# A two-block transformer kernel: vector products that move from TensorE to VectorE, low parts that move to GpSimd, and shorter waits in both mixers

## What is computed

```python
mod = silu(c) @ w_ada + b_ada                 # 2048 x 12288, per block
h = rms_norm(x, g) * (1 + scale1) + shift1
x = x + gate1 * (mixer(h @ w_in) @ w_out)     # block 1: retention, RWKV-7, MoBA
h = rms_norm(x, g) * (1 + scale2) + shift2    # block 2: Fourier mix, mLSTM both ways
u = depthwise_conv3(h @ w_up)                 # 2048 x 11264
x = x + gate2 * ((silu(gate) * value) @ w_down)
```

## Time and profile before

| | |
|---|---|
| runs (3), median, lowest to highest | 2574.45 us, 2573.42 to 2577.0 |
| the profiled execution: time, span | 2573.34 us, 2571.5 us |
| PE busy | 2504.7 us (97%) |
| DVE, ACT, POOL busy | 1410.7 (55%), 1121.8 (44%), 1227.0 (48%) us |
| DMA | 611.69 MB, mean 238 GB/s |
| mean granted clock of PE | 0.992 |

### The profile page before, as it was taken

How to read it: one execution, slowest core, us unless ns; L and a number is a source line. 1 busy time by engine, 2 the same in 40 slices (tenths; PEclk the granted TensorE clock), 3 DMA queues, 4 the chain that set the end, 5 groups by cost and what they waited for, 6 DMA issues and landing times.

```text
span 2571.5 us, 50484 instructions
## 1 busy us (share of the span) xinstructions
PE 2504.7 (97%) x19860; PEld 2284.6 (89%) x19860; DVE 1410.7 (55%) x2324; ACT 1121.8 (44%) x1316; POOL 1227.0 (48%) x500
## 2 busy tenths in 40 slices
PE   7999999999999999999999999999999999999997
PEld 5887887889999999998888877899999999998886
DVE  2535224465776777776665635345765756443333
ACT  2253324444444444444444444443544444444443
POOL 2663444665444444444444565466443444434442
...
GB/s 396 391 245 158 198 198 197 254 308 287 237 271 277 277 262 265 273 271 261 272 265 257 161 234 191 188 255 302 191 217 246 222 234 192 181 183 193 191 191 120
DMA packets 140382, 611.69 MB, mean 238 GB/s; under 512 B 15584, under 2 KB 15968, under 8 KB 115680
## 3 DMA queue, kind: packets, MB, share of 16 engines
...
...
## 4 chain that ended last, share of the span: by engine, by line
issue 45%; PE 32%; POOL 20%; DMA 1%; POOLq 1%; DVE 1%; ACT 0%; DVEq 0%; SPq 0%; ACTq 0%
PE psum L1927 32%; POOL wlo L1736 20%; DMA raw<-wstream 1%; POOLq L1733 0%; DMA ada_raw<-adastream 0%; DVE xT L2266 0%; POOLq L1735 0%; PE psum L2156 0%; ACT whi L1747 0%; DVE psum L2266 0%; DVE gslo L2258 0%; ACT arena L1750 0%; ACT gshi L1747 0%; POOLq L1736 0%; ACT arena L1747 0%
## 5 line engine op out<-in xcount | busy, mean ns | idle before, releaser
L1736 POOL TENSOR_TENSOR wlo<-raw,whi 128x1024 fp32r<-128x1024 f32 x496 | 1226.8, 2479 | 1315.7 <-ACT whi L1747 1314.8
L1747 ACT ACTIVATE whi<-raw 128x1024 fp32r<-128x1024 f32 x760 | 800.5, 1059 | 957.3 <-PE psum L1927 732.5
L1927 PE MATMUL psum<-hi_h,whi 128*128 128x256 f32 x4224 | 1207.1, 286 | 7.0 <-POOL wlo L1736 4.0
L1927 PE MATMUL psum<-hi_h,wlo 128*128 128x256 f32 x4224 | 1191.4, 282 | 0.0
L1927 PE MATMUL psum<-lo_h,whi 128*128 128x256 f32 x4224 | 1191.2, 282 | 0.0
L1927 PEld LDWEIGHTS psum<-hi_h,whi 128*128 128x128 f32 x4224 | 799.5, 189 | 20.0 <-issue 6.7
L1927 PEld LDWEIGHTS psum<-hi_h,wlo 128*128 128x128 f32 x4224 | 799.7, 189 | 1.9 <-issue 1.7
L1927 PEld LDWEIGHTS psum<-lo_h,whi 128*128 128x128 f32 x4224 | 799.4, 189 | 0.0
L2258 DVE TENSOR_TENSOR wlo<-raw,whi 128x1024 fp32r<-128x1024 f32 x264 | 378.6, 1438 | 280.1 <-ACT whi L1747 280.1
L2266 DVE SCALAR_TENSOR_TENSOR psum<-ada_raw,cact,psum 128x256 f32<-128x256 f32 x702 | 287.5, 481 | 15.5 <-DMA ada_raw<-adastream 15.4
L1927 PE MATMUL psum<-whi,gshi 128*128 128x512 f32 x704 | 276.7, 393 | 3.9 <-DVE gslo L2258 3.5
...
## 6 DMA issues: line engine op xcount, KB each, us to landing
raw<-wstream SPq DMA_DIRECT2D x760, 512.0 KB, 4.6
ada_raw<-adastream SPq DMA_DIRECT2D x168, 1024.0 KB, 7.1
arena<-adastream SPq DMA_DIRECT2D x24, 1024.0 KB, 17.7
xT<-x_in SPq DMA_DIRECT2D x8, 512.0 KB, 6.5
y_out<-xT SPq DMA_DIRECT2D x4, 512.0 KB, 2.6
gs_pages<-tabs_in SPq DMA_DIRECT2D x2, 512.0 KB, 4.3
gs_pages<-rw_in SPq DMA_DIRECT2D x2, 512.0 KB, 7.2
...
```

What stands on the lines that cost most here:

```text
L1736: nc.gpsimd.tensor_tensor(wlo[:, q, :], raw[:, q, :], whi[:, q, :].bitcast(F32), ALU.subtract).then_inc(sem.lo_ready, 1)
L1747: return nc.scalar.activation(out_, in_, ACT.Copy, scale=scale)
L1927: return nc.tensor.matmul(o, lhsT, rhs, start=start, stop=stop, skip_group_check=True)
```

## The change

- **Units in mixer 1.** `LOOP_UNITS` are units 19 to 26, two for each of the four turns. PE multiplies them no longer; DVE does, in `loop_products`, one instruction depending on the one before, in slices of 1 to 12 between the levels. PE keeps the `finish` of each.
- **Mixer 2 has none.** Its nine units are made in FFN 1 up, where nine of eleven turns (`UP_UNITS1`) now have three units. The three finishes of such a turn stand ahead of slab 6, ahead of slab 12, and at its end.
- **POOL makes all low parts of FFN 1 up**; DVE starts with FFN 1 down.
- **Waits.** Mixer 1: ACT makes two `whi` before it waits for the first low-rank product; MoBA's normalisation of four heads is shared by ACT (two) and DVE (two), and PE waits by head. A `fill(1)` moves from before the last `t_ready` to the end of the turn. Mixer 2: two slabs go ahead of the gates; the reciprocal and what follows it in a head use PSUM bank 6 in place of SBUF. Both FFNs: ACT and DVE split the first two chunks of the down product's input earlier.

```diff
-SPOTS2 = (12, 16, 20, 24, 32, 40, 48, 56, 64)
+LOOP_UNITS = (START_UNITS + 3, START_UNITS + 11)
+UP_UNITS1 = ((1, 2), (9, 3), (1, 2))
...
 def by_pe(u):
-    return u < MIX_UNITS1[1] or MIX_UNITS2[0] <= u < MIX_UNITS2[1]
+    return u < LOOP_UNITS[0] or LOOP_UNITS[1] <= u < MIX_UNITS1[1]
...
-    if n % 2 and (B1_UP <= n < B2 or n >= B2_UP):
+    if n % 2 and (B1_DOWN <= n < B2 or n >= B2_UP):
         return True, dve
...
                 scores_of(1, bank[6], 0, sem.sc2)
                 fill(1)
+                spot()
...
-                    if l == 2:
+                    if l == 4:
                         spot()
-                fill(1)
                 pe.wait_ge(sem.t_ready, 6 * t + 6)
...
                 ins.then_inc(sem.fh, 1)
-                spot()
+                fill(1)
...
             def moba_turn(n):
-                pe.wait_ge(sem.mo_p, n + 1)
                 for h in range(4):
                     o = bank[(6, 4, 5, 6)[h]]
+                    pe.wait_ge((sem.mo_p_act, sem.mo_p)[h // 2], 2 * n + 1 + h % 2)
...
             fn(halves(3)[:, 1, :], halves(3)[:, 1, :], ACT.Sigmoid).then_inc(sem.lora_act, 1)
+            his(G_TQK * GS + 3, G_TQK * GS + 5)
             act.wait_ge(sem.lora_pe, 1)
...
                     dve.wait_ge(sem.u_done, 5 * t + l)
                     if l < 5:
                         tt(MT, L1T, level(l + 1), ALU.mult).then_inc(*at.up(sem.mt))
-                    if l == 3:
-                        unit_rows()
+                    loop_products(*{1: (2 * t, 0, 3), 2: (2 * t, 5, 8), 3: (2 * t, 10, 13), 4: (2 * t, 15, 16),
+                                    5: (2 * t + 1, 0, 4)}[l])
                     dve.wait_ge(sem.d_done, 5 * t + l)
...
+                    loop_products(*{1: (2 * t, 3, 5), 2: (2 * t, 8, 10), 3: (2 * t, 13, 15), 4: (2 * t, 16, 16),
+                                    5: (2 * t + 1, 4, 16)}[l])
...
+            slot(1, 0)
             pe.wait_ge(sem.wg_ready, 1)
...
             ins.then_inc(sem.gates, 1)
-            slot(1, 0)
             slot(1, 1)
+            slot(1, 2)
 
             pe.wait_ge(sem.gt_ready, 1)
...
-                    tt(inv, inv, bank[5], ALU.max).then_inc(*at.up(sem.step))
+                    tt(inv, least, bank[5], ALU.max).then_inc(*at.up(sem.step))
                     dve.wait_ge(*at.last)
                     V.reciprocal(inv, inv).then_inc(*at.up(sem.step))
                     dve.wait_ge(*at.last)
-                    for n, (pp, jb, q, d) in enumerate(PARTS):
-                        tt(pp, pp, inv[:, d * S + q.start:d * S + q.stop], ALU.mult).then_inc(*at.up(sem.step))
+                    fwd0, bwd1 = inv[:, 0:S], inv[:, S:2 * S]
+                    tt(pf0, pf0, fwd0, ALU.mult).then_inc(*at.up(sem.step))
...
-                        if t == NFF - 1 and half == 1:
+                        if t == NFF - 1 and half == 0:
                             for kk in range(2):
                                 gs_hi(n0 + more * NFF, b, kk)
...
+                            if units == 3 and k == (6, 4)[half]:
+                                finish(0, units * per, 0 if i is None else i)
...
+            def loop_products(n, k0, k1):
+                u = LOOP_UNITS[0] + n
+                for kt in range(k0, k1):
+                    s, k = divmod(kt, 8)
+                    if k == 0:
+                        dve.wait_ge(sem.ada_landed[s], 16 * (u - START_UNITS + 1))
+                    w, c = ada_raw[:, s, k * 256:(k + 1) * 256], cact[:, kt:kt + 1]
+                    if kt == 0:
+                        dve.wait_ge(sem.ada_sum, u)
+                        ts(sums_of(0), w, c, None, ALU.mult).then_inc(*at.up(sem.step))
+                    else:
+                        dve.wait_ge(*st["sum"])
```

More of the change, by code:

```diff
@@ L134, in ada_places @@
         first = spots[u - units[0] - 1] + 4 if u > units[0] else spot - 6
+        late = LOOP_UNITS[0] <= u < LOOP_UNITS[1] and (u - LOOP_UNITS[0]) % 2
         for s in range(2):
-            at.setdefault(n0 + first + s, []).append((u, s))
+            at.setdefault(n0 + first + s * (2 if late else 1), []).append((u, s))
     return at
@@ L153, in lo_per @@
 def lo_per(n, per):
-    return per if n < B1_UP or B2 <= n < B2_UP else per // 2
+    return per if n < B1_DOWN or B2 <= n < B2_UP else per // 2
 def tables():
@@ L928, in moba_exp @@
                             ins.then_inc(sem.mo_exp, 1)
+                act.wait_ge(sem.mo_inv, n + 1)
+                for h in range(2):
+                    for ib in range(2):
+                        s = mscores[:, h, P * ib:P + S * ib]
+                        c = 8 + 4 * ib + h
+                        ins = copy(s, s, scale=small[:, c:c + 1])
+                        if ib:
+                            ins.then_inc(sem.mo_p_act, 1)
             def moba_turned(n, h):
@@ L1127, in moba_norm @@
                 dve.wait_ge(sem.mo_exp, n + 1)
-                V.reciprocal(small[:, 8:16], small[:, 8:16]).then_inc(*at.up(sem.step))
+                V.reciprocal(small[:, 8:16], small[:, 8:16]).then_inc(*at.up(sem.mo_inv))
                 dve.wait_ge(*at.last)
-                for h in range(4):
+                for h in range(2, 4):
                     for ib in range(2):
@@ L1133, in moba_norm @@
                         c = 8 + 4 * ib + h
-                        ts(s, s, small[:, c:c + 1], None, ALU.mult).then_inc(*at.up(sem.mo_p if h == 3 and ib else sem.step))
+                        ts(s, s, small[:, c:c + 1], None, ALU.mult).then_inc(*at.up(sem.mo_p if ib else sem.step))
             moba_bias(0)
@@ L1206, in build, with pe_mix2 @@
         mask_f, mask_b = page(20)[:, S:2 * S], page(20)[:, 0:S]
-        def pe_mix2(pe, st, mm, product, part, spot):
+        def pe_mix2(pe, st, mm, product, part):
             def slot(g, s):
@@ L1705, in _ @@
             out_slabs(B1_OUT + GS, B1_UP, at_out, {B1_OUT + GS + (0, 3, 9, 16)[k]: functools.partial(x_again, k) for k in range(4)})
-            groups(B1_UP, NFF, {3: 0, 6: 1, GS + 3: 0, GS + 6: 1}, 2 * GS)
+            at = B1_UP
+            for turns, units in UP_UNITS1:
+                groups(at, turns, {3: 0, 6: 1, GS + 3: 0, GS + 6: 1} if units == 2 else
+                       {1: 0, 3: 1, GS: 0, GS + 2: 1, GS + 4: 0, GS + 7: 1}, 2 * GS)
+                at += 2 * GS * turns
             down(B1_DOWN, True)
@@ L2021, in spot @@
                 if u == u1:
+                    return
+                if not by_pe(u):
+                    st["unit"] += 1
                     return
@@ L2240, in _ @@
             output(B1_OUT, MIX1, 1, 0, (sem.mix_split, 0, 2))
-            up(B1_UP, 0, 8, [(NFF, 2)])
+            up(B1_UP, 0, 8, UP_UNITS1)
             down(B1_DOWN, 0, 2, 4, True)
             st["free"] = {0: (sem.x_ready, 8), 1: (sem.x_ready, 8)}
-            st.update(unit=MIX_UNITS2[0], units=MIX_UNITS2, spots=SPOTS2, slabs=0, after_taken={MIX_UNITS2[0]: 10})
-            pe_mix2(pe, st, mm, product, part, spot)
+            st["slabs"] = 0
+            pe_mix2(pe, st, mm, product, part)
             output(B2_OUT, MIX2, 4, 12, (sem.mix_split, 4, 2))
@@ L2345, in unit_rows @@
                     rows(u - 1)
+            def loop_products(n, k0, k1):
[10 more added lines that the diff above has]
+                        dve.wait_ge(*st["sum"])
+                        at.n[sem.ada_used] = u
+                        stt(acc[:, 0, 0, :] if kt == KT - 1 else sums_of(0), w, c, sums_of(0), ALU.mult, ALU.add
+                            ).then_inc(*at.up(sem.ada_used if kt == 7 else sem.acc_ready if kt == KT - 1 else sem.step))
+                    st["sum"] = at.last
+                if k1 == KT and k1 > k0:
+                    st["spot"] = u + 2
             def norm0():
@@ L2453, in ffn @@
                     first, last = done == 0, done == NFF - 1
-                    with at.loop(dve, turns, {sem.lo2_ready: GS - first, sem.gs_lo: 2 * last, sem.cw_ready: 1, sem.free_val: 1, sem.free_gate: 1,
+                    lo2s = GS - first if lo_signal(n0 + 1)[0] else 2 if last else 0
+                    with at.loop(dve, turns, {sem.lo2_ready: lo2s, sem.gs_lo: 2 * last, sem.cw_ready: 1, sem.free_val: 1, sem.free_gate: 1,
                                                 sem.g_made: 1, sem.acc_ready: units, sem.ada_used: units,
@@ L2472, in ffn @@
-                            if has:
-                                if uu - 1 not in (MIX_UNITS1[1] + OUT_UNITS - 1, MIX_UNITS2[1] + OUT_UNITS - 1):
-                                    modulation(uu - 1, per=units, i=i)
-                                st["marks"] = {0: at.last, 1: at.last}
-                            if half == 1:
-                                quarter_unit(0, 0)
-                            lo2(lo_at + 2, 2 * GS, i)
-                            if half == 0:
-                                quarter_unit(0, 0)
@@ L2481, in ffn @@
-                            quarter_unit(0, 1)
-                            lo2(lo_at + 4, 2 * GS, i)
```

(8 more changed lines are left out.)

115 lines of the change are left out of this document (65 added, 50 removed).

## The result

| | before | changed | ratio, 95% interval |
|---|---|---|---|
| median of 4 runs each | 2575.16 us | 2547.79 us | 0.9893, 0.9876 to 0.9911 |
| profiled execution: time, span | 2573.34, 2571.5 | 2548.8, 2547.0 | |

A forecast was written before the change was run, and what follows sets the result against it. PE, busy 97% of the span, bounds the kernel, so time goes when work or idle time leaves PE. Gains 62.7 less losses 7.8 give 54.9; 2574.4 - 54.9 = 2519.5, stated as 2519 us, range 2508 to 2546.

The forecast's parts named there:

- Units off PE, 31.3 us: Both mixers: seventeen units leave PE, eight of mixer 1 and nine of mixer 2, at 1.84 us each; gain 31.3 us.
- Waits in mixer 1, 5.7 + 4.7: Mixer 1: slab 36's low-part wait and slow clock go, 5.7 us; two waits for MoBA's normalised scores go, 4.7.
- the products there, 2.3: Mixer 1: DVE's products fit its idle time; only PE's smaller cover for the last step costs, 2.3 us.
- The heads' 8.0 us: Mixer 2: three heads' waits, 2.7 us each, go because the reciprocal in PSUM shortens DVE's chain by some 4.5; gain 8.0.
- The gates, 6.3 us: Mixer 2: the gates' product no longer waits 2.9 us for its weights' low part, nor loses 3.4 to half clock.
- rival 2: Both mixers: the waits change place and half of PE's 24.7 us idle time stays; 2531 to 2536 us, chance 0.12.
- each edit takes off more than the wait that it meets: Mixers: argument against waits changing place, citing 4.5 us against 2.7 and 3.9 against 4.0.
- Slacks of 0.2 to 1 us, met three times a turn: I take 0.5 us a turn, 9 x 0.55 = 5: FFN 1 up: tight places in the order of nine three-unit turns cost small delays, a loss of 5 us.
- None of them is full, so none becomes the bound: FFN 1 up, three units: DVE near 31 of 46 us, POOL 39.7 of 46.4, DMA share 0.88; none limits.
- The gain of 1.5 us that I had taken for the first finish: FFN 1 up: the first finish's wait of 1.47 us for DVE goes, as DVE is free earlier; gain 1.5.
- Rival 1: FFN 1 up: POOL's low parts hold DVE, PE stops about 2 us a turn, 17 us in nine; 2536 us, chance 0.22.
- FFN 2, 3.6 us: FFN 2: earlier splits remove the down product's wait for `gslo`, 1.9 us, and 1.7 of slow clock behind it.

The follow-up runs named there:

- the last two versions: Changed kernel with units' places moved and DVE making the first turn's odd low parts, 2522.99 us; the same plus two edits in mixer 2, 2516.34 us.
- the last one: Changed kernel with units' places moved, DVE making the first turn's odd low parts, and ACT's high parts and DVE's scaling of x earlier in mixer 2: 2516.34 us.

## Why the prediction was wrong

- **Units off PE, 31.3 us: right.** 1.84 us a unit holds: eight of them back on PE cost 13.6 to 16 us.
- **Waits in mixer 1, 5.7 + 4.7, and the products there, 2.3 (with 0.5 for the scaling): right, a little too cautious.** Mixer 1 and its output gave 25.8 for 22.3. The cover lost before the last step cost nothing that can be seen.
- **The heads' 8.0 us: right, and by its mechanism.** The six operations fell to 1.7 us, under the 2.8 that I worked out, and undoing the edit in the changed kernel cost mixer 2 all of it and the clock's part, 13 us.
- **The gates, 6.3 us: the step that names rival 2.** The wait for `wgs` went, but ACT still waited for DVE's memset before its next high part, and slab 409 was 2.6 us late in its place. With the chain of row operations (2.7 and 3.4 of clock) mixer 2 gave 26.7 for 35.0 (my own "some 245" us for it should have read 243 by those terms). I had written that each edit takes off more than the wait that it meets (it did not even hold for my own 3.9 against 4.0); what stood next in ACT's order, and what DVE's chain would meet when seventeen us of PE's work had gone from beside it, I had not looked up. I also misread the edit: what it moves ahead of the gates is two slabs, 48 matmuls, not half a slab with 12. That covers the wait for `wgs`, and one of the two slabs is the late one.
- **"Slacks of 0.2 to 1 us, met three times a turn: I take 0.5 us a turn, 9 x 0.55 = 5": this step failed.** The nine turns lost 2.1 us each beside their own sum, 19 us in all, 14 more than the term. "None of them is full, so none becomes the bound" was right of the engines and the DMA, and two of the three places were named. The slacks were the error. I counted DVE's gate product at 1.23 us where it took 1.70, had PE free for the sum 0.5 us too late, slab 8's transfer out 0.5 too early and landed in 5.6 for 6.3, and took ACT's mean over all its operations (0.82) for a high part that takes 1.06. The sum and slab 8 were each 0.9 us late, and slab 15 I had not worked out. With the places moved by one slab the nine turns take 46.9 us, and the 19 us are back.
- **A term was missing altogether.** I read rows 10 in the middle of the stage, and asked POOL only whether it had time. In the first turn DVE splits the normalised input from two SBUF operands, and POOL, now twice as busy, held it: 8.8 us, and 9 us on the kernel before by itself. The gain of 1.5 us that I had taken for the first finish lay in the same turn and did not come either: even with DVE's low parts back, PE waits 1.44 us there. These 10 us and the 14 above are the 24 by which FFN 1 up misses its column. Rows 8 showed the same price in mixer 2, and I used it there.
- **Rival 1 was the nearer story**: GpSimd holds DVE in FFN 1 up. Its mechanism is shown, its place was not the costly one: in the three-unit turn above POOL took 0.5 us from the gate product, not 2.4, and unit 0 was complete at +17.3, not +19.2; in the run with the places moved that product takes 1.22 again. Its sign, a turn over 48.5, came true mostly by the slacks, and its time, 2536, was still 12 us short. The rule of the Trainium skill (page "SBUF — State Buffer", section "Who interferes with whom") covers the place that I missed as well: `lo_h` has two SBUF inputs, the products have one. The trace agrees in both: 0.87 us becomes 3.00 for two of `lo_h`, and thirteen products take 5.18 us, 0.40 each, while POOL works without a break (924.32 to 934.44). I weighed the rule at one operation, instead of asking it of all that DVE does beside POOL.
- **FFN 2, 3.6 us: 2.1.** `gslo` is no longer waited for and the clock no longer falls, but DVE's two earlier splits (`gslo`, 3.50 us at 2266.62) now stand ahead of a low part near the end of the up product, and that one is 1.3 us late (the wait for `wlo` above).

What stays open: whether SP's places alone give back the 19 us of FFN 1 up, why two turns with three units took 0.5 to 1 us more than the rest in each of the last two versions, and why the first turn took 49.7 us in the last one for 48.4.
